# 44 passes instead of 47, and GpSimd arithmetic instead of accumulating DMAs and VectorE adds, in the down projection of a decoder layer

## The reference, cut to what matters

```python
def _layer(x, ...):
    xn = _rmsnorm(x, p['n_mix_pre'])
    mix, ... = _mixer(xn, ...)            # GLA and SSD heads, one output projection
    x = x + _rmsnorm(mix, p['n_mix_post'])
    xn = _rmsnorm(x, p['n_ffn_pre'])
    f, f_new = _conv_ffn(xn, s_ffn, p)
    return x + _rmsnorm(f, p['n_ffn_post']), ...

def _conv_ffn(xn, s_ffn, p):
    u = xn @ p['ffn_w_in']                # 2048 -> 2 x 5632
    u, buf = _causal_dwconv(u, s_ffn, p['ffn_conv_w'], p['ffn_conv_b'])
    a, b = jnp.split(u, 2, axis=-1)
    return (jax.nn.silu(a) * b) @ p['ffn_w_out'], ...   # g @ w_out: 5632 -> 2048
```

## Time and profile before

| | |
|---|---|
| median of 3 runs | 2520.68 us (2518.03 to 2522.0) |
| the profiled execution | 2520.21 us, its span 2518.4 us |
| busy in the span: PE / DVE / ACT / POOL | 2445.3 / 1875.0 / 1099.0 / 424.9 us |
| mean granted TensorE clock | 0.989 of full speed |

### The profile page before, as it was taken

How to read it: one execution, slowest core, us unless ns; L and a number is a source line. 1 busy time by engine, 2 the same in 40 slices (tenths; PEclk the granted TensorE clock), 3 DMA queues, 4 the chain that set the end, 5 groups by cost and what they waited for, 6 DMA issues and landing times.

```text
span 2518.4 us, 48870 instructions
## 1 busy us (share of the span) xinstructions
PE 2445.3 (97%) x20078; PEld 2411.2 (96%) x20078; DVE 1875.0 (74%) x2820; ACT 1099.0 (44%) x1702; POOL 424.9 (17%) x246
## 2 busy tenths in 40 slices
PE   7999999999999999989999999999999999999996
PEld 7999999999999999989999999999999999999995
DVE  6544545766146258898888898888899897798887
ACT  5332222433224235444444444444444665555542
POOL 3333222433223344000000000000000000000005
PEclk9999999999999999999999999999999999999997
DMA  5222227622273424233333333333333465656663
GB/s 177 89 82 90 81 93 265 235 75 68 94 270 119 154 71 152 87 101 104 107 107 109 114 113 104 107 107 109 113 114 120 139 162 159 170 143 174 167 175 110
DMA packets 103246, 322.96 MB, mean 128 GB/s; under 512 B 11120, under 2 KB 15856, under 8 KB 102144
## 3 DMA queue, kind: packets, MB, share of 16 engines
q1 hardware_dynamic: 58336, 211.84, 26.6%
q10 hardware_dynamic: 39232, 88.60, 9.9%
q0 software_dynamic: 5472, 19.61, 4.5%
HBM read 255.77 MB, written 44.62 MB: 119 GB/s over the span
## 4 chain that ended last, share of the span: by engine, by line
PE 64%; issue 15%; DVE 10%; POOL 4%; DMA 4%; ACT 2%; POOLq 0%; ACTq 0%; DVEq 0%; SPq 0%
PE psum_proj L1412 10%; PE psum_proj L1913 7%; PE psum_proj L1915 7%; PE psum_proj L1914 7%; PE psum_work L1913 7%; PE psum_work L1915 7%; PE psum_work L1914 7%; PE psum_proj L1414 5%; POOL w_lo L609 4%; DMA raw<-in_weights_dram 3%; PE psum_work L1412 1%; DVE w_lo L2567 1%; PE psum_work L1414 1%; DVE arena L2833 1%; DVE arena L2483 1%
## 5 line engine op out<-in xcount | busy, mean ns | idle before, releaser
L1412 PE MATMUL psum_proj<-x_hi,w_hi 128*128 128x288 f32 (+2 forms) x1696 | 510.7, 301 | 15.0 <-DVE x_lo L2064 12.9
L1412 PE MATMUL psum_proj<-x_lo,w_hi 128*128 128x288 f32 (+2 forms) x1696 | 500.9, 295 | 0.0
L1414 PE MATMUL psum_proj<-x_hi,w_lo 128*128 128x288 f32 (+2 forms) x1696 | 500.6, 295 | 0.0
L609 POOL TENSOR_TENSOR w_lo<-raw,w_hi 128x1024 fp32r<-128x1024 f32 x128 | 321.6, 2515 | 619.1 <-ACT w_hi L705 619.1
L705 ACT ACTIVATE w_hi<-raw 128x1024 fp32r<-128x1024 f32 x138 | 145.2, 1056 | 484.8 <-PE psum_proj L1414 406.5
L1412 PEld LDWEIGHTS psum_proj<-x_hi,w_hi 128*128 128x128 f32 x1696 | 320.6, 189 | 22.3 <-issue 15.5
L1412 PEld LDWEIGHTS psum_proj<-x_lo,w_hi 128*128 128x128 f32 x1696 | 319.8, 189 | 2.7 <-issue 1.9
L1414 PEld LDWEIGHTS psum_proj<-x_hi,w_lo 128*128 128x128 f32 x1696 | 319.5, 188 | 0.0
L666 POOL DMA_DIRECT2D arena<-m_stage x38 | 32.9, 869 | 1425.3 <-ACT m_stage L1241 1424.6
L1913 PE MATMUL psum_proj<-ops_a,w_hi 128*128 128x288 f32 x808 | 241.5, 299 | 15.3 <-DVE arena L2823 9.1
L1915 PE MATMUL psum_proj<-ops_a,w_lo 128*128 128x288 f32 x808 | 240.0, 297 | 0.0
(11 more groups left out here) (463 smaller groups left out, 6836.2 us busy)
## 6 DMA issues: line engine op xcount, KB each, us to landing
raw<-in_weights_dram SPq DMA_DIRECT2D x386, 512.0 KB, 3.6
g_spill<-x_flat ACTq DMA_DIRECT2D x44, 288.0 KB, 2.1
arena<-m_stage POOLq DMA_DIRECT2D x19, 576.0 KB, 5.6
x_flat<-g_spill ACTq DMA_DIRECT2D x17, 576.0 KB, 6.0
arena<-m_stage POOLq DMA_DIRECT2D x19, 432.0 KB, 8.4
spill<-tail ACTq DMA_DIRECT2D x24, 288.0 KB, 2.1
arena<-in_xT_dram SPq DMA_DIRECT2D x4, 1152.0 KB, 10.6
y_spill<-arena ACTq DMA_DIRECT2D x4, 1152.0 KB, 4.9
```

The lines of the kernel that those rows point to most:

```text
L609: nc.gpsimd.tensor_tensor(w_lo[:, slot], raw[:, r], w_hi[:, slot].bitcast(F32), ALU.subtract).then_inc(lo_ready, 1)
L1412: nc.tensor.matmul(banks[:, n, 0:b - a], w_hi[:, slot, k], (hi, lo)[part][:, a:b], start=first and part == 0, stop=False)
L1414: mm = nc.tensor.matmul(banks[:, n, 0:b - a], w_lo[:, slot, k], hi[:, a:b], start=False, stop=last)
```

## The change

The table `WINDOWS` is another one, with 44 passes instead of 47 (the 168 steps are the same in number). All passes after the first of a pair, except the last two, are staged by ScalarE as before (34 instead of 37), and each is added by two GpSimd `tensor_tensor` instructions in place of the accumulating DMA or the VectorE add. `add_stage` is gone from VectorE. The last two passes belong to pairs j = 2 and 3; `combine(2)` is now run by GpSimd, after its adds. `combine(3)` takes the place of `combine(6)` in the last part; VectorE has the other six inside the loop. `LAST_TILES` starts with the tiles of pairs 4 to 7. The loads of h are issued two tiles at a time, in fewer DMAs, and a little later.

```diff
-WINDOWS = ((2, 3, 4, 3, 5, 4), (2, 3, 5, 3, 4, 4), (2, 3, 4, 5, 4, 3), (2, 4, 4, 5, 3, 3), (3, 4, 4, 4, 3, 3),
-           (3, 3, 5, 4, 3, 3), (4, 4, 3, 5, 3, 2), (4, 4, 4, 4, 5))
+WINDOWS = ((2, 3, 4, 5, 3, 4), (2, 4, 4, 4, 3, 4), (2, 5, 3, 5, 3, 3), (2, 5, 4, 4, 3, 3), (3, 5, 4, 4, 5),
+           (3, 5, 4, 4, 5), (4, 5, 4, 3, 5), (5, 4, 4, 3, 5))
-LAST_TILES = (14, 15) + tuple(range(14))
-BY_VE = (len(PASSES) - 2, len(PASSES) - 1)
-STAGED = [p for p, (r, j, first, stop) in enumerate(PASSES) if r and p not in BY_VE]
-BY_DMA, VE_ADDED = STAGED[0::2], STAGED[1::2]
-ADDED_AT = {END_STEP[p] // 2 + 1: p for p in VE_ADDED}
+LAST_TILES = tuple(range(8, 16)) + tuple(range(8))
+LATER = [p for p, (r, j, first, stop) in enumerate(PASSES) if r]
+BY_VE = LATER[-2:]
+STAGED = [p for p in LATER if p not in BY_VE]
...
 # GpSimd
-            for p in BY_DMA:
+            for p in STAGED:
                 j = PASSES[p][1]
                 for half, (first, stop) in enumerate(((0, M_SPLIT), (M_SPLIT, 7))):
                     pool.wait_ge(*product_out(p, stop - 1))
-                    for before in added_before(p):
-                        pool.wait_ge(*stage_added(before, half))
-                    pool.dma_start(m_of(j, first, stop), m_stage[:, first * HALF:stop * HALF], accum_op=ALU.add)\
-                        .then_inc(m_acc[half], 16)
+                    pool.wait_ge(*added_before(p, half))
+                    m = m_of(j, first, stop)
+                    nc.gpsimd.tensor_tensor(m, m, m_stage[:, first * HALF:stop * HALF], ALU.add).then_inc(m_acc[half], 1)
+            def combine(j):
...                                # the same five tensor_tensor as VectorE's, with waits on pool_step
+            combine(2)
...
 # ScalarE
                         if q in (0, M_SPLIT):
-                            act.wait_ge(*(stage_added(STAGED[before - 1], q // M_SPLIT) if before else (op_low, G_OPS0 + 1)))
+                            act.wait_ge(*((m_acc[q // M_SPLIT], before) if before else (op_low, G_OPS0 + 1)))
...
-                if w > H_FREED and w - H_FREED - 1 < 7:
+                if w > H_FREED:
                     act.wait_ge(units_done, W_UNIT0 + H_FREED + 1)
-                    h_load(w - H_FREED + 2, w - H_FREED + 3)
+                    first = 3 + 2 * (w - H_FREED - 1)
+                    h_load(first, min(first + 2, H_FIRST))
...
 # VectorE
-            def add_stage(p, half):
...
-                if added is not None:
-                    add_stage(added, 0)
...
-                if added is not None:
-                    add_stage(added, 1)
...
-                for j in combined_at.get(w, ()):
-                    if w >= ALL_UNITS - 1:
-                        settle()
-                    combine(j)
+                if w in combined_at:
+                    combine(combined_at[w])
+                if w == ALL_UNITS - 1:
+                    tail_lows(2)
...
-            take_pass(BY_VE[1])
-            tail_lows(2)
+            take_pass(BY_VE[-1])
...
                 if e == 6:
-                    combine(6)
+                    combine(3)
                     settle()
+                if e == 11:
+                    ve.wait_ge(pool_step, 5)
```

More of the change, by code:

```diff
@@ L383, in build @@
         H_FIRST = 10
-        fsum, fsum_v = A(2016 * 7, 576), A(0, 576)
-        fsq = [A(2016 * (1 + i), 576) for i in range(3)] + [w_sum_b[:, 0:576]]
+        fsum, fsum_v = A(2016 * 4, 576), A(2016 * 5, 576)
+        fsq = [A(2016 * i, 576) for i in (6, 7, 0)] + [w_sum_b[:, 0:576]]
         const_in = sem("const_in")
@@ L484, in product_out, with added, added_before @@
             if p in BY_VE:
[L485 to L496, removed]
+                return taken, DOWN_TAKEN0 + 7 * BY_VE.index(p) + q + 1
+            return part_out, FT - STD + 7 * (p - sum(i < p for i in BY_VE)) + q + 1
+        def added(p, half):
+            if p in STAGED:
+                return m_acc[half], STAGED.index(p) + 1
+            return product_out(p, M_SPLIT - 1 if half == 0 else 6)
+        def added_before(p, half):
+            return added([i for i in range(p) if PASSES[i][1] == PASSES[p][1]][-1], half)
         HALF_TILES = 4
@@ L544, in build @@
         TAIL_FREED, H_FREED = (WUNITS + LAST_USE[kp] // 2 for kp in (16, 17))
[L545 to L547 removed]
+        combined_at = {min(WUNITS + END_STEP[p] // 2 + 3, ALL_UNITS - 1): j for j, p in enumerate(LAST_PASS)
+                       if p not in BY_VE[-2:]}
         L = BATCHES - LATE_B
@@ L663, in _ @@
                     pool.wait_ge(*product_out(p, stop - 1))
-                    for before in added_before(p):
-                        pool.wait_ge(*stage_added(before, half))
-                    pool.dma_start(m_of(j, first, stop), m_stage[:, first * HALF:stop * HALF], accum_op=ALU.add)\
-                        .then_inc(m_acc[half], 16)
+                    pool.wait_ge(*added_before(p, half))
+                    m = m_of(j, first, stop)
+                    nc.gpsimd.tensor_tensor(m, m, m_stage[:, first * HALF:stop * HALF], ALU.add).then_inc(m_acc[half], 1)
+            def combine(j):
+                p = LAST_PASS[j]
+                m = m_of(j).rearrange("p (n t) -> p n t", n=7)
+                for half in range(2):
+                    pool.wait_ge(*added(p, half))
+                nc.gpsimd.tensor_tensor(m[:, 2:4], m[:, 2:4], m[:, 0:1].broadcast_to([P, 2, HALF]), ALU.add)\
+                    .then_inc(pool_step, 1)
+                pool.wait_ge(pool_step, 1)
+                nc.gpsimd.tensor_tensor(m[:, 0], m[:, 1], m[:, 3], ALU.subtract).then_inc(pool_step, 1)
+                pool.wait_ge(pool_step, 2)
+                nc.gpsimd.tensor_tensor(m[:, 1], m[:, 3], m[:, 5], ALU.subtract).then_inc(pool_step, 1)
+                pool.wait_ge(pool_step, 3)
+                nc.gpsimd.tensor_tensor(m[:, 3], m[:, 6], m[:, 1], ALU.add).then_inc(pool_step, 1)
+                nc.gpsimd.tensor_tensor(m[:, 4:6], m[:, 4:6], m[:, 0:1].broadcast_to([P, 2, HALF]), ALU.add)\
+                    .then_inc(pool_step, 1)
+            combine(2)
             def square_sum(n, kt):
@@ L2816, in take_pass @@
                 j = PASSES[p][1]
-                for before in added_before(p):
-                    for half in range(2):
-                        ve.wait_ge(*stage_added(before, half))
+                for half in range(2):
+                    ve.wait_ge(*added_before(p, half))
                 for q in range(7):
@@ L2823, in take_pass @@
                     tt_op(m, bank(7 * p + q), m, ALU.add).then_inc(taken, 1)
-            def add_stage(p, half):
[L2827 to L2832, removed]
-                tt_op(m, m_stage[:, first * HALF:stop * HALF], m, ALU.add).then_inc(taken, 1)
             def combine(j):
@@ L2838, in combine @@
                 m = m_of(j).rearrange("p (n t) -> p n t", n=7)
-                if p in BY_VE:
-                    ve.wait_ge(*product_out(p, 6))
-                else:
-                    for half in range(2):
-                        ve.wait_ge(*stage_added(p, half))
+                for half in range(2):
+                    ve.wait_ge(*added(p, half))
                 own(tt_op(m[:, 2:4], m[:, 2:4], m[:, 0:1].broadcast_to([P, 2, HALF]), ALU.add))
```

8 lines of the change are left out of this document (4 added, 4 removed).

## The result

The changed kernel takes 2576.78 us (median of 4 runs, 2573.83 to 2578.41), the kernel before in the same job 2521.34 (2518.03 to 2523.03). The ratio is 1.0226, 95% interval 1.0212 to 1.0241: slower by 2.3%, or 55.4 us. The forecast was 2576 us.

What follows compares the result with a forecast made beforehand. TensorE bounded the kernel, busy 2445.3 of 2518.4 us; VectorE would become the bound. 37.9 us of VectorE overrun plus 18 us of remaining idle time on 2520.2 gave 2576 us, 8 in 10 between 2553 and 2612.

Steps and rivals of the forecast that it cites:

- VectorE's own work, 315.5 us: Down projection's loop: VectorE's work falls from 360.4 to 315.5 us, losing 36 adds and a combine, gaining a tail low.
- GpSimd holds VectorE for 150.7 us: Down projection's loop: 34 passes at 4.31 us hold VectorE 146.5 us, and combine(2) 4.2 us more.
- VectorE becomes the bound: Down projection's loop: VectorE occupied 466.2 us against the stretch's 428.3 and TensorE's 405.6, costing 37.9 us.
- A quarter of the idle time stays, 18 us: Down projection's loop: of VectorE's 67.9 us idle time, about 18 us comes on top; weight waits shrink.
- DMAs gone, ScalarE 0: Staging: accumulating DMAs and some ScalarE copies go, but nothing counts while VectorE is late; cost 0, -3 to +3 us.
- End wait about 6 us: Loop's end: TensorE's 9.13 us wait for VectorE's combines falls to about 6, with nothing added to the sum.
- The table 0, the last part 0: Before 2034 us, new table costs 0, at most 3 us; after 2462.3, cost 0, at most 2 us either way.
- The sign that failed: Profile after: TensorE's waits would name VectorE's low parts, 40 to 70 us, ScalarE's small; mainly ScalarE would refute the forecast.
- The high end of the main range: Whole kernel: 2600 us as top of the main case, from two thirds of idle time left plus the page's price.
- The adds hidden: Rival, down projection's loop: GpSimd's adds fall into VectorE's idle time or do not hold it; 2503 us, chance 0.05.
- Half hidden: Rival, down projection's loop: VectorE held only in part, some 120 us instead of 151; 2526 to 2553 us, chance 0.07.
- The clock on top: Rival, down projection's loop: waits drop TensorE to half clock, adding 58 us, half exposed; 2600 to 2635 us, chance 0.15.

Runs made afterwards that it cites:

- All by VectorE: Changed kernel with all 34 staged passes added by VectorE itself instead of GpSimd: 2517.66 us, 0.9991 of the kernel before.
- memsets: Changed kernel with a GpSimd memset of the same accumulator columns in place of each add: 2497.55 us, 0.9909 of the kernel before.
- all by DMA: Changed kernel with all 34 staged passes added by accumulating DMAs from GpSimd's queue: 2526.77 us, 1.0024 of the kernel before.
- 8 columns: Changed kernel with each GpSimd add cut to 8 columns, all waits kept: 2496.26 us, 0.9909 of the kernel before.
- copy: Changed kernel with a GpSimd copy of the staged columns in place of each add: 2502.74 us, 0.9929 of the kernel before.
- old routes: Changed kernel with staged adds as in the kernel before, 17 by accumulating DMA and 17 by VectorE: 2530.86 us, 1.0049 of the kernel before.
- old table: Changed kernel with the 47-pass table put back, GpSimd adding all 37 staged passes: 2585.28 us, 1.0265 of the kernel before.
- a quarter by DMA: Changed kernel with every fourth staged pass by accumulating DMA, others by VectorE: 2513.55 us; same with the 47-pass table: 2520.66 us.

## Why the prediction was right, point by point

1. *VectorE's own work, 315.5 us.* Confirmed to within 10 us. All by VectorE has 398.2 us with 34 adds of 2.40: 398.2 - 81.6 = 316.6, `combine(2)`'s hold still in it. Where VectorE adds nothing and only `combine(2)` can hold it, it is busy for 328.1 us (memsets), 325.6 (all by DMA) and 324.2 (8 columns); less 4.2 these are 320 to 324. The difference is in part that VectorE's instructions overlap by some 0.08 us when they follow each other at once (four banks of 0.44 us took 1.54), which a waiting VectorE does less.
2. *GpSimd holds VectorE for 150.7 us.* Right in kind (memset, copy, columns), a little too large: 452.4 - 315.5 = 136.9 us. Less 4.2 for `combine(2)` that is 1.95 us an add instead of 2.16 (against the memsets' 328.1 us, `combine(2)` included, it is 124.3 us or 1.83 an add). Part of the adds meets VectorE's waits or its PSUM work, or starts within an instruction.
3. *VectorE becomes the bound.* Right. It is busy for 93% of the stretch, and the two parts of the length that moved are its own: busy time +92.0 us, idle time -32.9 (67.9 to 35.0), together the +59.1 of the stretch. The forecast had +105.8 and -49.9. That the sum (+56 to +59) came so near is in part luck: the two terms were off by 14 and 17 us in opposite directions.
4. *A quarter of the idle time stays, 18 us.* It was 35. The DMA waits fell as foretold, from 46.5 to 10.8 us; not foreseen were the other 24 us, nearly all for ScalarE, 12.9 of them for its high parts of g (L2822). Such waits stand there before too (67.9 - 46.5 = 21 us) and in each kernel that does all the adds (13 to 34 us). With GpSimd's adds in place of the old routes that share shrank by less than the waits for DMAs did: with the new table from 27 us to 24, with the old table from 21 to 13. Why it stays is not shown; ScalarE and VectorE hand g and weights back and forth.
5. *DMAs gone, ScalarE 0.* No gain was seen; ScalarE's own waits for VectorE make it the bearer of the delay.
6. *End wait about 6 us.* 5.4, and 2.5 more for the banks of the last but one pass.
7. *The table 0, the last part 0.* The last part lost 1.2 us. The table at 0 was wrong as a general price: it costs 12 us with the old routes and 3 with VectorE alone, and gains 7 with a quarter by DMA and 8.5 to 10.7 with GpSimd's adds. In the changed kernel, where VectorE's sum sets the time, it did no harm.

The sign that failed is the name in TensorE's waits, and the prediction had set it down as a sign of being wrong ("if TensorE waits mainly for ScalarE"). Forecast: VectorE's low parts with 40 to 70 us, ScalarE small. Measured: 30.7 us for ScalarE's copies, 10.5 for VectorE's operands of g (L2822), 487.4 - 429.0 = 58 in all. For 9.3 us of these ("issue") the profile names no releaser; a share of them may be waits for low parts. So the step from VectorE to TensorE was foreseen along the wrong path. The row of ScalarE's waits settles whose lateness it was: 203 us behind the weight sums, 105 before. ScalarE's program has those sums' high parts ahead of the pass's copies, so a late sum blocks the bank before it blocks a low part.

The high end of the main range does not follow from its words: 2558 and two thirds of 67.9 are 2603, and 15 more are 2618, not 2600. The result does not depend on it.

The rivals. The adds hidden: excluded. But its case was seen where hardly anything holds VectorE: with 8 columns or memsets the kernel takes 2496 to 2498 us (2503 forecast). Half hidden: excluded by the time, though the held time of 129 to 137 us lies between its 120 and the forecast's 151; the idle time that stayed made up for it. The clock on top: in the loop, by the records of the granted clock, TensorE ran at half clock for 52.3 us against 14.9, and its busy time rose by 23.4 us (half of the 37.4 more, 18.7 us, is the most that the clock can have added). Yet 429.0 stays below VectorE's 452.4. How much of the +59 would go with a full clock was not isolated, since no kernel here changes the clock alone; VectorE's busy and idle time account for the whole without it, but some of the waits for ScalarE may be its echo.

## What to carry to other kernels

Add up what occupies the second-busiest engine: its own work, what a neighbour's instructions hold it for, and its waits for transfers. Here that sum cost about 0.3 us per us while it was below the bounding engine's time, and about one to one above it. Price each route of an operation in that engine's time: a staged pass costs VectorE 2.40 us when it adds itself, about 3.9 when GpSimd adds (3.8 by the pair of kernels that differ in 17 passes), and about 2 in waits when a DMA accumulates ((73 - 7) / 34), but lumped and hard to foretell (1.3 and 2.9 a pass with nine such passes in the two tables). "Moved to an idle engine" is no gain as long as the busy one is held. When the profile names an engine as releaser, look at what that engine waited for before.

## Of the hardware, not expected

- A GpSimd memset of 1152 columns (1.06 us) beside VectorE work with two SBUF inputs leaves it at 1.215 to 1.227 us; a one-input copy of the same piece (1.38 us) lengthens it to 2.17.
- The more passes go by accumulating DMA, the longer VectorE waits for loads of other queues: 3 to 11 us with none, 18 to 29 with 9, 47 to 53 with 17 or 19, 73 with 34.
- The hold goes both ways. A GpSimd add of 8 columns takes 0.22 us in the median of 68, and up to 1.61; of the 22 above 0.32 us, 21 end 0.06 us behind the end of a VectorE instruction with two SBUF inputs. One of 1152 columns takes 2.69 us at the least and 2.93 in the mean, one of 864 columns 2.06 and 2.53. The least are the forecast's 2.68 and 2.05.
